# Mixer loop: small products made in bursts of four chunks, half of z and r made on GpSimd, the shift of v and the bonus product moved later

## The reference, cut to what matters

```python
def rwkv7_step(state, inp):
    r, decay, k, v, kk, a = inp
    sa = jnp.einsum('bhij,bhj->bhi', state, -kk)
    state = (state * decay[:, :, None, :]
             + sa[..., None] * (kk * a)[:, :, None, :]
             + v[..., None] * k[:, :, None, :])
    out = jnp.einsum('bhij,bhj->bhi', state, r)
    return state, out
...
    kk = kk / jnp.maximum(jnp.sqrt(jnp.sum(kk * kk, axis=-1, keepdims=True)), 1e-12)
    ...
    bonus = jnp.sum(r * k * r_k.astype(f32), axis=-1, keepdims=True) * v
```

## Time and profile before

| | us |
|---|---|
| median of three runs | 3747.55 |
| lowest, highest | 3739.74, 3748.70 |
| the profiled execution | 3741.37 |
| its span from first to last instruction | 3739.5 |
| TensorE busy in the span | 3509.0 |
| VectorE, ScalarE, GpSimd busy | 1643.4, 1166.4, 489.3 |
| one fill, f = 2 | 13.93 |
| one turn of the loop, f = 1 | 123.6 |

### The profile page before, as it was taken

One profiled execution on the slowest core, in us unless ns is written; L12 is line 12 of the kernel. 1 busy time (PEld: TensorE's weight loads), 2 busy tenths in 40 slices (PEclk: granted clock), 3 DMA queues, 4 the chain that ended last, 5 costly groups with the idle time before them and its releaser, 6 DMA issues.

```text
span 3739.5 us, 56748 instructions
## 1 busy us (share of the span) xinstructions
PE 3509.0 (94%) x24253; PEld 2008.9 (54%) x24253; DVE 1643.4 (44%) x2561; ACT 1166.4 (31%) x2075; POOL 489.3 (13%) x475
## 2 busy tenths in 40 slices
PE   8899999989779998989999999998998999899999
PEld 4465565565433333445556555555554666566654
DVE  2454555454321113723545544454224655455541
ACT  1333333321011112433333333342213444344430
POOL 0222122111000001301101010010102100200000
PEclk9999999989879998999999999999999999999999
DMA  3000000031379989910000000021200000000001
GB/s 111 24 18 19 19 13 24 13 116 58 112 302 354 392 315 350 344 36 18 18 18 1 18 18 18 12 74 61 80 6 12 1 1 13 3 22 1 1 23 68
DMA packets 99777, 290.16 MB, mean 78 GB/s; under 512 B 12886, under 2 KB 38806, under 8 KB 86342
## 3 DMA queue, kind: packets, MB, share of 16 engines
q1 hardware_dynamic: 79750, 236.10, 17.3%
q0 software_dynamic: 6912, 25.17, 1.9%
q10 hardware_dynamic: 12864, 25.27, 1.9%
HBM read 342.56 MB, written 38.32 MB: 102 GB/s over the span
## 4 chain that ended last, share of the span: by engine, by line
PE 83%; DVE 8%; DMA 3%; ACT 2%; issue 2%; SPq 1%; POOL 1%; ACTq 0%; DVEq 0%; POOLq 0%
PE ps L2678 11%; PE ps L2124 8%; PE ps L403 8%; PE ps L2153 7%; PE ps L3390 7%; PE ps L1696 5%; PE ps L2696 4%; PE ps L1184 3%; PE ps L3662 3%; PE ps L3071 3%; PE ps L1716 2%; PE ps L3343 2%; DMA sb<-in_exp_up 2%; PE ps L2362 1%; PE ps L499 1%
## 5 line engine op out<-in xcount | busy, mean ns | idle before, releaser
L2678 PE MATMUL ps<-sb 128*128 128x512 f32 x960 | 466.1, 605 | 19.6 <-ACT sb L2036 10.9
L2124 PEld LDWEIGHTS ps<-sb 128*128 128x128 f32 x2624 | 288.6, 141 | 303.9 <-ACT sb L2132 130.0
L2124 PE MATMUL ps<-sb 128*128 128x128 f32 x2624 | 417.9, 282 | 19.5 <-DVE sb L2140 9.6
L2132 ACT ACTIVATE sb<-ps 128x512 f32<-128x512 f32 x336 | 200.1, 597 | 716.6 <-PE ps L2124 716.6
L2098 ACT ACTIVATE sb<-ps,sb 128x1280 f32<-128x1280 f32 (+1 forms) x288 | 353.2, 1231 | 130.7 <-DVE sb L2091 112.2
L2140 DVE COPY sb<-ps 128x512 f32<-128x512 f32 x320 | 220.0, 689 | 376.7 <-PE ps L2124 376.2
L403 PE MATMUL ps<-sb 128*128 128x512 f32 x704 | 353.4, 619 | 4.6 <-DMA sb<-in_w_in 3.0
L3390 PE MATMUL ps<-sb 96*128 96x512 f32 (+1 forms) x768 | 332.2, 525 | 9.0 <-DVE sb L3447 7.2
L2153 PEld LDWEIGHTS ps<-sb 128*64 128x64 f32 x5248 | 287.6, 138 | 70.8 <-issue 40.4
L2153 PE MATMUL ps<-sb 128*64 128x128 f32 x5248 | 322.2, 277 | 3.3 <-DVE sb L2140 3.1
L1919 POOL TENSOR_TENSOR sb<-sb 128x1 f32<-128x1 f32 (+3 forms) x114 | 131.9, 1158 | 1071.1 <-DVE sb L1915 1071.0
(11 more groups left out here) (369 smaller groups left out, 4573.3 us busy)
## 6 DMA issues: line engine op xcount, KB each, us to landing
sb<-in_exp_gate SPq DMA_DIRECT2D x64, 1024.0 KB
sb<-in_exp_up SPq DMA_DIRECT2D x64, 1024.0 KB
sb<-in_exp_down SPq DMA_DIRECT2D x64, 1024.0 KB
sb<-in_l_w_mod ACTq DMA_DIRECT2D x12, 2048.0 KB, 13.6
d_ys<-sb SPq DMA_DIRECT2D x64, 256.0 KB
sb<-d_x SPq DMA_DIRECT2D x32, 512.0 KB, 3.8
sb<-in_w_in SPq DMA_DIRECT2D x22, 512.0 KB, 4.2
sb<-in_x SPq DMA_DIRECT2D x16, 512.0 KB, 4.5
```

The lines of the kernel that those rows point to most:

```text
L2124: ins = k.pe.e.transpose(k.bank(bank)[:, 128 * j:128 * j + 128], self.Pb[g % 2][:, 1280 * b + 128 * c:1280 * b + 128 * c + 128], k.f(C_ID, ...
L2132: k.act.e.activation(self.PT[:, xs[0]:xs[-1] + 1, :], k.bank(bank)[:, 0:128 * len(xs)].rearrange("p (j t) -> p j t", j=len(xs)), ACT.Copy) ...
L2678: ins = pe.e.matmul(k.bank(5), lhs[:, kk, :], w[:, kk, 512 * half:512 * half + 512], start=kk == 0, stop=kk == 7)
```

## The change

- **Fill.** The product bT x z leaves step `ab` and becomes a step of its own, `zb`: for four chunks at a time, 16 products on 64x64 tiles (only the blocks of the triangle that are used), all in banks 6 and 7. ScalarE copies each bank in one piece, 128x512, where it took four small pieces a chunk. Order: ab 0, zb 0, ab 1, then ab 2 and 3 with two transposes, zb 1, ab 4 to 7 with two transposes.
- **Copies.** The transposed b and k are copied by ScalarE alone; VectorE keeps one half of v.
- **z and r.** The second half of `zr` is made by GpSimd. The sign of z moves into two other operations (`ctr_kn`, `scaled_b`).
- **v.** The shift of v on VectorE (735) leaves its place in front of the fill and becomes a step `shift_v`; its wait for ScalarE's copy stays where it was. `shift_v` and `rk` are now the first steps of the tail, which so has two steps more; `rk` leaves its place behind the fill.

```diff
     def fill(f):
-        return weave([("ab", c) for c in range(8)], [("tail_turn", f, n) for n in range(4)])
+        return ([("ab", 0), ("zb", 0), ("ab", 1)] + weave([("ab", 2), ("ab", 3)], [("tail_turn", f, 0), ("tail_turn", f, 1)])
+                + [("zb", 1)] + weave([("ab", c) for c in range(4, 8)], [("tail_turn", f, 2), ("tail_turn", f, 3)]))
 
     def tail(f):
-        return [("bonus", f, 0), ("bonus", f, 1)] + [("tail_turn", f, n) for n in (4, 5)] + [("tail_end", f)]
+        return [("shift_v",), ("rk", f), ("bonus", f, 0), ("bonus", f, 1)] + [("tail_turn", f, n) for n in (4, 5)] + [("tail_end", f)]
...
-        order += [("zr", f, 1)] + fill(f) + [("rk", f)]
+        order += [("zr", f, 1)] + fill(f)
...
+        elif kind == "zb":
+            half, = x
+            pe.wait_ge(*t["zr", half])
+            pe.wait_ge(*t["bT"])
+            pe.wait_ge(*free[6])
+            pe.wait_ge(*free[7])
+            for c in range(4 * half, 4 * half + 4):
+                for r in range(2):
+                    for h in range(2):
+                        of_t = slice(128 * (c % 4), 128 * (c % 4) + (64 if r else 128))
+                        ins = pe.e.matmul(k.bank(6 + h)[halves[r ^ h], of_t], bT[halves[h], 128 * c + 64 * r:128 * c + 64 * r + 64],
+                                          zr[halves[h], c, 0, 64 * r:128], start=True, stop=True, skip_group_check=True)
+            ins.then_inc(*product.up())
+            t["zbmm"] = product.at
...
-            for h in range(2):
-                pe.wait_ge(*free[6 + h])
-                ins = pe.e.matmul(k.bank(6 + h)[:, 0:128], bT[halves[h], cs], zr[halves[h], c, 0, :], start=True, stop=True)
-            ins.then_inc(*product.up())
-            t["zbmm"] = product.at
...
+        elif kind == "zb":
+            half, = x
             act.wait_ge(*t["zbmm"])
...
+            for h in range(2):
+                act.e.activation(zb[half].rearrange("p (c h) t -> p h c t", h=2)[:, h], k.bank(6 + h).rearrange("p (c t) -> p c t", c=4), ACT.Copy).then_inc(*evac_a.up())
+                free[6 + h] = t["zb", half] = evac_a.at
...
+        elif kind == "shift_v":
+            dve.wait_ge(*t["unshifted"])
+            dve.e.scalar_tensor_tensor(out=vT, in0=raw[:, 0:1024], scalar=t["v_scale"], in1=vT, op0=ALU.mult, op1=ALU.add).then_inc(*shifted.up())
+            t["raw"] = t["vT"] = shifted.at
...
+        elif kind == "zr" and x[1] == 1:
+            cs = slice(4, 8)
+            pool.wait_ge(*t["ex"])
+            pool.wait_ge(*t["kn"])
+            pool.wait_ge(*t["ym", 1])
+            pool.e.tensor_tensor(zr[:, cs, 0, :], c8(T[2])[:, cs, :], c8(T[0])[:, cs, :], ALU.mult)
+            pool.wait_ge(*t["ep"])
+            pool.wait_ge(*t["shift", "rm"])
+            pool.e.tensor_tensor(zr[:, cs, 1, :], c8(rm)[:, cs, :], c8(T[3])[:, cs, :], ALU.mult).then_inc(*pool_out.up())
+            t["zr", 1] = pool_out.at
```

## The result

| | before | after |
|---|---|---|
| median, us | 3745.19 (6 runs) | 3766.01 (6 runs) |
| lowest, highest | 3739.74, 3750.08 | 3757.93, 3774.05 |
| profiled execution, its span | 3741.37, 3739.5 | 3764.93, 3763.1 |
| TensorE busy in the span | 3509.0 | 3517.0 |
| a turn of the loop, f = 1 to 4 | 123.59, 123.57, 125.20, 123.57 | 129.64, 129.66, 129.66, 129.66 |

The ratio is 1.0055, with a 95 % interval of 1.0036 to 1.0074. The time of 3766.0 lies on the upper edge of the predicted range (3736 to 3766), 14.5 us above the predicted time: the change is slower by more than the 0.3 % that this kernel's runs can tell. It was the mechanism of rival 2 that came, not the likeliest case, and it cost a little more than the 3760 to 3764 that rival 2 had.

What follows compares the result with a forecast made beforehand. TensorE was taken as the bound, four fifths and more of the chain of waits. Four turns +3.3, clock +4.8, first turn -4.1, last turn 0 gave +4 us: 3751.5 on the median, range 3736 to 3766.

Steps and rivals of the forecast that it cites:

- rival 2: Each new stand, behind the bonus and at the scan's start, costs its own slow-clock stretch: 3760 to 3764 us; chance 0.2.
- The fill: Start of each mixer turn: chunks made in bursts of four take 11.1 us against 13.93, so -2.8 (-3.3 to -1.4).
- the eight groups at 0.76: In the fill: eight groups L462/L465 at 0.76 us each make 6.1 us of its 11.1.
- Rival 3: In the fill: the burst isn't packed, its four quadrants take turns, 1.6 us a burst; 3760 us; chance 0.1.
- What hides zr on GpSimd: Before the fill: POOL idles, so zr's second half is done by 384.6, needed about 388; uncovered it would cost 2.5 us.
- The merges: After the fill, turns 1 to 4: rk no longer precedes the merges, but VectorE waits for L575 anyway; -0.1 us.
- The bonus: Tail of turns 1 to 4: it now stands behind both merge_b and needs the late rk; a new wait of 1.9 us.
- The decay: Tail of turns 1 to 4: two projection steps now precede the lora product; the scan's waits grow by 1.8 us.
- The clock: One stretch at TensorE's lower clock in each of four turns, three more than before: +4.8 us (0 to 11).
- The first turn: Turn f = 0: -1.2 before the fill, -2.0 in it, -0.9 in the merges; together -4.1 us (-5.5 to -2.5).
- The last turn: Turn f = 5: fill -2.8, later merge_b 3 +2.3, half a us for clock; net about 0 (-2 to +2).

Runs made afterwards that it cites:

- the experiment with one product: Kernel with rk and v's shift out of the tail in turns 1 to 5, plus one unused product before the first scan_s of turns 1 to 4: 3724.37 us, ratio 0.9949.
- the first experiment: The change, but with rk and the shift of v taken out of the tail in turns 1 to 5: 3730.38 us, ratio 0.9970 to the kernel before.

## Why the prediction was right in its waits and short in its size

The time fell on the edge of the range, and that is luck more than merit: the forecast was +4 in the trace and +26.4 came in the mixer loop. The waits were foreseen well; the number of slow stretches and the last turn were not.

**The fill**: -2.8 was said (-3.3 to -1.4), -1.96 came. The waits were right (0.50 and 0.50 for 0.55 and 0.35). The mis-sized term is the eight groups at 0.76: they add up to 6.59 instead of 6.1, and the bursts are 1.02 instead of 0.9. The rows above show why: a group between a burst and another group takes 0.76 (386.81 to 387.57), one between two transposes 0.86 (388.90 to 389.76). The bursts bring three more changes of tile shape into each fill (11 for 8), and I had counted them in the burst only, and not in the groups. A change costs about 0.1. The Trainium skill (TensorEngine Tiling (Array Packing), Key Properties) says that such a change drains the engine; the trace shows a cost that fits it, this 0.1, and can't show the draining itself. Rival 3 did not come: 16 products of 1536 columns in 1.02 are packed.

**What hides zr on GpSimd**: right; 1.27 and 1.09, done 5 us early. Without the move a fill is 0.43 longer.

**The merges**: -0.1 was said, -0.10 came (1.20 for 1.30).

**The bonus**: a new wait of 1.9 was said, 2.06 came, at L842 as said, and 0.18 behind it. **The decay**: 1.8 was said, with part of it at scan_r; 1.37 + 0.28 - 0.46 = 1.2 came. The waits named as signs were 1.4 at scan_r and 1.9 at scan_s; 1.37 and 1.60 came. The term that I missed is that kk's sum then waits 0.46 less. The tail with the merges cost +3.33 where +3.6 was said.

**The clock is the step that failed.** One slow stretch a turn of 1.6 was taken, 4.8 over all; there were two, one behind the bonus (some 1.9) and one at the scan (some 2.8), 4.7 a turn, 18.8 less the 1.6 that was there before, 17.2 over all. That is even more than rival 2 had (11.2), since the scan's stretch was longer after waits of 1.37 and 1.60 (some 2.8) than after one of 1.32 (1.4 to 1.7). The evidence against rival 2 was weak: "the wait of 1.3 did this in one turn of four only" was read as rarely, but the waits to come were longer, and stood closer, as the prediction itself says (1.4 and 1.9 within 4 us). It also put the bonus's wait "ten us earlier"; the rows of the change have 316.22 and 335.74, nearly twenty, and between them the clock was full again (L519 x16 at 0.68), so the two could not be one stretch. What I had in front of me also had the 0.83 at kk's sum, 1.5 us behind the 1.32, which the earlier trace rows doesn't show and I didn't weigh; the experiment with one product shows that with 0.47 in place of the 1.32 the stretch did not come. Whether the 1.32 alone would make it was not tried.

**The first turn**: its start was to gain 1.2 and lost 0.5. L735's 1.28 did go: the wait for VectorE there is 4.87 for 6.06. But the projections in front of it ended later, since the loads at the kernel's start landed later in this execution (the first projection, L404, starts at 24.73, before at 23.78) and the first 128 records of the projections took 58.21 for 57.48. I put this down to chance: over the kernels here the first fill starts between 137.9 and 140.1, whatever they change. The turn gained 4.3 (-2.9 was said, in two terms), 1.9 of it in the fill.

**The last turn**: 0 was said (-2 to +2), +7.5 came. merge_b 3 was placed too early: it starts 45.1 us after the fill's first product, before 43.0; without the fill's gain of 2.0 that is +4.1 where 1.7 to 2.3 was said. The difference shows in two rows: the two bonus products (four records) took 3.78 at half clock, and rk 2.29 rather than the 1.93 that I took as the upper bound. Then the stand of 5.01 came where 2.19 had been, and the clock was lower: from merge_b 3 to the first scan product the view by windows gives 28.44 us at a granted 0.74, before 23.13 us at 0.85. So the last turn lost 2.1 up to merge_b 3, with the fill's gain in it, and 5.3 behind, of which 2.8 are the longer stand. I had half a us for the clock here.

L842 and GpSimd's masks together took from 810.36 to 814.98, 4.62, with VectorE's shift before; alone they take 1.28, 1.27 and 2.51, 5.06. So there was almost no overlap. The Trainium skill (SBUF — State Buffer, SBUF: two separate sides) has these two lock each other out for a whole instruction, which would give the whole 5.06; the trace agrees but for 0.4.

**Sum.** With the measured terms: four turns of -1.96 + 3.33 are +5.5, the clock +17.2, the first turn and start -3.8, the last +7.5: +26.4, where the prediction had +4. The medians differ by 20.8 and the profiled spans by 23.6; the rest varies behind the mixer: from the first scan product of f = 5 to the end of the span, where no edit changes an instruction, the traces of the ten kernels take 2908.6 to 2923.3. The range reached to 3766 because the clock was in it with up to 11 us; the clock alone took 17.2. The chance of 0.2 for rival 2 rested on the reading of "one turn of four", and by what is said above it was too low.

## What to carry to other kernels

A step that is put at the head of a woven list costs more than its own time: it shifts every later step of that list, and here two steps that do nothing took back the whole gain of a shorter fill. Leave what is moved out of the weave, and put it in at a fixed place.

When TensorE is the bound, count its stands in clusters, and price the slow stretch behind them as well as the stands: here the new waits were 3.4 us a turn and the slow clock 4.7. If the wait can't be removed, an unused product in front of it, shorter than the wait, costs nothing and can give the clock back; here it was worth 1.4 us in each of three turns of the trace.

## What the runs showed of the hardware

- Short stands suffice to lower TensorE's clock, and the same stands don't always do it. Behind 2.06, mostly with 0.18 after it, it fell in all 12 turns of the change, of the kernel with the decay's projections put back and of the one with only the last turn's tail restored, but in one of four of the kernel with the new tail alone. Behind 1.37, 1.60 and 0.36 (to 0.83) it fell in all of the 16 turns of the four kernels that have them. Behind 1.32 and 0.83 it fell in one of four of the kernel before, and in three of four of the first experiment, of the kernel with zr on VectorE and of the one with the decay's projections put back. Behind 0.31, 0.74 and 0.83 it fell in two of four; behind 0.47 and 0.83 in none of four. Each of these counts is from one execution.
- A slow stretch cost 1.4 to 1.7 us behind the short stands of the scan, 1.6 to 1.9 behind the bonus, and some 2.8 behind the long stands of the scan in the change (1.6 to 3.1 over the kernels that have them), though TensorE had full work again at once.
- 16 products on 64x64 tiles (eight of 128 columns, eight of 64, f32) take 1.02 us; a change of tile shape costs about 0.1.
- In the merges of the last turn TensorE stood 2.0 to 5.0 us at one place (in two kernels 0.9 to 2.3 at each of two places) with nothing to wait for in the profile, and the length differed between kernels. Why stays open.
